# Up products of a ConvFFN: the convolution's accumulators in PSUM, another order at the entrance, and a product's low part moved from GpSimd to VectorE

## The reference

```
h2 = rmsnorm(x1) * (1 + sc2) + sh2              # 576 x 2048
u  = h2 @ w_up                                  # 576 x 11264
uc = depthwise_conv3(u_hist) + b_dw_f           # 3 taps, history in front of each sequence
y  = x1 + gt2 * ((silu(gate) * val) @ w_down)   # gate, val = the two halves of uc
```

## Time and profile before

| | us |
|---|---|
| median of 3 runs | 2999.72 |
| lowest and highest | 2998.53, 3000.04 |
| the profiled execution, its own time | 3009.53 |
| its span, first to last instruction | 3007.6 |

### The profile page before, as it was taken

The page is one execution under the profiler, slowest core; times in us unless marked ns, Lnnn a source line. Parts: engine busy times, 40 slices in busy tenths (PEclk is TensorE's granted clock), DMA queues, the critical chain, the costliest instruction groups (busy, mean ns, idle before and its releaser), DMA issues.

```text
span 3007.6 us, 52667 instructions
## 1 busy us (share of the span) xinstructions
PE 2814.1 (94%) x20368; PEld 2547.5 (85%) x20368; DVE 1940.0 (65%) x3011; ACT 1084.7 (36%) x2012; POOL 1708.9 (57%) x1894
## 2 busy tenths in 40 slices
PE   5798889999989879998899999999999989999999
PEld 2296478888964559997899999999999989999998
DVE  2225369999877543226888988998899843434342
ACT  2212323332214432125555555555555522121212
POOL 0134354444330064457799999999999954544453
PEclk8999999999989889998999999999999999999999
DMA  8832156552258683441333333333333453233323
GB/s 284 279 85 81 39 172 186 180 165 64 73 176 291 194 256 106 128 128 42 96 111 109 98 104 112 108 98 105 113 106 98 123 185 112 98 116 101 114 80 99
DMA packets 473921, 391.94 MB, mean 130 GB/s; under 512 B 29416, under 2 KB 402820, under 8 KB 473092
## 3 DMA queue, kind: packets, MB, share of 16 engines
q1 hardware_dynamic: 462914, 363.24, 39.4%
q0 software_dynamic: 8704, 19.27, 2.1%
q10 hardware_dynamic: 2075, 6.34, 0.7%
HBM read 363.85 MB, written 25.66 MB: 130 GB/s over the span
## 4 chain that ended last, share of the span: by engine, by line
PE 58%; POOL 19%; DVE 12%; DMA 4%; issue 3%; ACT 3%; ACTq 0%; SPq 0%; DVEq 0%; POOLq 0%
PE ps L1976 17%; POOL wlo L926 16%; PE ps L1428 15%; PE ps L2008 14%; DMA raw<-in_w_ada 3%; PE ps L1462 3%; DVE yb L2274 2%; DVE ye L2277 2%; POOL wlo L931 2%; POOL wlo L877 1%; ACT whi L1294 1%; DVE prod L2258 1%; DVE scP L2185 1%; PE ps L1887 1%; PE ps L1840 1%
## 5 line engine op out<-in xcount | busy, mean ns | idle before, releaser
L926 POOL TENSOR_TENSOR wlo<-raw,whi 128x256 fp32r<-128x256 f32 x672 | 764.0, 1169 | 82.6 <-ACT whi L1294 82.5
L877 POOL TENSOR_TENSOR wlo<-raw,whi 128x256 fp32r<-128x256 f32 (+1 forms) x424 | 370.3, 904 | 482.8 <-ACT whi L976 482.8
L931 POOL TENSOR_TENSOR wlo<-raw,whi 128x256 fp32r<-128x256 f32 x352 | 277.0, 819 | 296.3 <-ACT whi L1318 296.3
L2008 PE MATMUL ps<-XH,whi 128*128 128x288 f32 x1344 | 409.6, 305 | 15.2 <-POOL wlo L926 10.0
L1428 PE MATMUL ps<-XH,whi 128*128 128x288 f32 (+1 forms) x1760 | 390.7, 303 | 18.2 <-POOL wlo L877 16.8
L2008 PE MATMUL ps<-XH,wlo 128*128 128x288 f32 x1344 | 398.1, 296 | 0.0
L2008 PE MATMUL ps<-XL,whi 128*128 128x288 f32 x1344 | 398.0, 296 | 0.0
L2008 PE MATMUL ps<-x1R,whi 128*128 128x288 f32 x1344 | 396.5, 295 | 0.0
L1428 PE MATMUL ps<-XL,whi 128*128 128x288 f32 (+1 forms) x1760 | 378.6, 296 | 0.0
L1428 PE MATMUL ps<-XH,wlo 128*128 128x288 f32 (+1 forms) x1760 | 378.2, 296 | 0.0
L1294 ACT ACTIVATE whi<-raw 128x512 fp32r<-128x512 f32 x420 | 263.9, 629 | 269.3 <-PE ps L2008 178.9
(11 more groups left out here) (379 smaller groups left out, 6348.2 us busy)
## 6 DMA issues: line engine op xcount, KB each, us to landing
raw<-in_w_ada SPq DMA_DIRECT2D x192, 512.0 KB, 4.8
raw<-in_w_up SPq DMA_DIRECT2D x176, 512.0 KB, 4.0
raw<-in_w_down SPq DMA_DIRECT2D x88, 512.0 KB, 3.4
raw<-in_w_in SPq DMA_DIRECT2D x68, 512.0 KB, 5.4
Vp<-in_cache_v POOLq DMA_DIRECT2D x128, 128.0 KB, 4.0
raw<-in_w_out SPq DMA_DIRECT2D x32, 512.0 KB, 3.9
raw<-in_cache_k SPq DMA_DIRECT2D x64, 128.0 KB, 2.3
g32a<-g_far SPq DMA_DIRECT2D x6, 1152.0 KB
```

The costliest lines, as they stand in the source:

```text
L877: last = G.tensor_tensor(l[:, a:a + width // 4], raw_of(u, m)[:, a:a + width // 4], h[:, a:a + width // 4].bitcast(F32), ALU.subtract)
L926: last = G.tensor_tensor(lp[:, a:a + 256], src[:, a:a + 256], hp[:, a:a + 256].bitcast(F32), ALU.subtract)
L931: last = G.tensor_tensor(wlo[:, d % 2, a:a + 256], raw[:, d % 4, a:a + 256], whi[:, d % 2, a:a + 256].bitcast(F32), ALU.subtract)
L2008: ins = mm(dst, wt, x(4 * h + k), start=h + k == 0 and wt is a and x is xh, stop=h == 1 and k == 3 and wt is b)
```

## The change

- The accumulators of the convolution move from SBUF (`four`) to PSUM: two banks for v = 0 (4 and 5), two for v = 1 (6 and 7). The last tap of the gate row goes from PSUM to SBUF (`vals`), where Silu and the gate read it; the value row is read by the gate from PSUM.
- The seven products now share banks 0 to 3, so `product` waits for other readers. The copy p5 of product 1 is gone: VectorE reads bank 1.
- The low part of product 6 moves from GpSimd to VectorE, between `gate_rows` and `gate`. The count of GpSimd's low parts per pair goes from 10 to 8 halves wherever it is waited for.
- At the entrance ScalarE makes the high parts 6 and 7 of the plain products ahead of the evacuations, VectorE's `operand_forms` wait until GpSimd has made the low part 7, the first high half of product 0 goes ahead of the copies of the forms, and SyncE loads slots 0, 1, 2, 3 in this order.
- Left out below: the same change of counts in two waits of SyncE and one of TensorE, and other bank numbers in the state rows, the down stage and the output's transposes (the down stage's first tile now uses banks 0 and 1, with a wait for the last value rows).

```diff
-        p5 = at(o_c + 8 * TB + TB // 2, "p5", [128, TH])
...
-        gout = [four[:, 2 * CV:2 * CV + T], rstd[:, :]]
+        gout = [four[:, CV:CV + T], four[:, CV + T:CV + 2 * T]]
...
-        conv = [four[:, v * CV:v * CV + CV - 2] for v in range(2)]
+        vals = four[:, 0:CV - 2]
...
+        def conv(v):
+
+            return ps_all[:, 4 + 2 * v:6 + 2 * v, :].rearrange("p a c -> p (a c)")[:, 0:CV - 2]
...
-        POOL_LO, DVE_LO = (0, 2, 3, 5, 6), (1, 4)
+        POOL_LO, DVE_LO = (0, 2, 3, 5), (1, 4, 6)
...
             if p in DVE_LO:
-                return s_lod.at(4 * i + 2 * DVE_LO.index(p) + h + 1)
-            return s_lo, W0 + 10 * i + 2 * POOL_LO.index(p) + h + 1
+                return s_lod.at(6 * i + 2 * DVE_LO.index(p) + h + 1)
+            return s_lo, W0 + 8 * i + 2 * POOL_LO.index(p) + h + 1
...
-            for s in (3, 2, 0, 1):
+            for s in range(4):
                 block(0, s)
...
             def taps(f, v):
                 ch = f + v * FT
-                w(act, s_gt, f)
+                if v:
+                    w(act, s_gt, f)
+                elif f:
+                    act.wait_ge(s_c3, conv_count(f - 1, 0))
                 bias, tap = vT[:, 2, ch:ch + 1], vT[:, 5, ch:ch + 1]
-                A.activation(conv[v], cin[:, v, 0:CV - 2], ACT.Identity, bias=bias, scale=tap).then_inc(s_t0, 1)
+                A.activation(conv(v), cin[:, v, 0:CV - 2], ACT.Identity, bias=bias, scale=tap).then_inc(s_t0, 1)
                 last_rows_of(f, v)
...
-            def snap(i, which):
-
-                act.wait_ge(*product_done(i, which))
+            def snap(i):
+
+                act.wait_ge(*product_done(i, 0))
                 if i:
-                    act.wait_ge(*(s_u4 if which else s_c11).at(i))
-                    if which:
-                        act.wait_ge(*s_cv[1].at(i))
-                A.activation((p1, p5)[which][:, :], bank(which, 128, 0, TH), ACT.Copy).then_inc(s_snap.sem, 1)
+                    act.wait_ge(*s_c11.at(i))
+                A.activation(p1[:, :], bank(0, 128, 0, TH), ACT.Copy).then_inc(s_snap.sem, 1)
...
-                A.activation(conv[0], conv[0], ACT.Silu).then_inc(s_gl, 1)
+                A.activation(vals, vals, ACT.Silu).then_inc(s_gl, 1)
...
             hi(u, 4, 2)
+            hi(u, 6)
             up_evac(u, 2, 0, 0, 0)
+            hi(u, 7)
+            up_evac(u, 3, 0, 0, 1)
             silu_gate(0)
-            up_evac(u, 3, 0, 0, 1)
-            hi(u, 6)
-            hi(u, 7)
             up_evac(u, 5, 0, 1, 0)
-            act.wait_ge(s_form.sem, s_form.done + 4)
+            form_hi(0, 0, 0)
+            act.wait_ge(*s_form.at(3))
             form_rows(0, x1T[:, 0:8, 0:TH], T1h[:, :, :])
-            form_hi(0, 0, 0)
+            act.wait_ge(*s_form.at(4))
             form_rows(1, x1T[:, 8:16, 0:TH], T4h[:, :, :])
             silu_gate(1)
...
-                snap(i, 0)
+                snap(i)
...
-                snap(i, 1)
...
-                dst = bank((0, 1, 2, 3, 6, 7, 4)[p], 128, 0, TH)
-                if p < 2:
-                    pe.wait_ge(*(s_snap.at(2 * i - 1 + p) if i else (s_uv, 3)))
+                dst = bank((0, 1, 2, 3, 0, 3, 2)[p], 128, 0, TH)
+                if p == 0:
+                    pe.wait_ge(*(s_q.at(2 * i) if i else (s_uv, 3)))
+                elif p == 1:
+                    pe.wait_ge(*(s_u4.at(i) if i else (s_uv, 3)))
                 elif p == 2:
-                    pe.wait_ge(*(s_cv[1].at(i) if i else (s_uv, 4)))
+                    pe.wait_ge(*(s_cv[0].at(i) if i else (s_uv, 4)))
+                elif p == 3:
+                    w(pe, *s_c11.at(i))
+                elif p == 4:
+                    pe.wait_ge(*s_snap.at(i + 1))
                 elif p == 5:
-                    w(pe, *s_c11.at(i))
-                elif p == 6:
-                    w(pe, *s_cv[0].at(i))
+                    pe.wait_ge(*s_q.at(2 * i + 1))
+                else:
+                    pe.wait_ge(*s_cv[1].at(i + 1))
                 if i == 0 and 1 <= p <= 4:
...
             def operand_forms():
 
+                dve.wait_ge(s_lo, Tally(U_FFN).index(7) + 1)
                 TT(b11, b12, b11, ALU.subtract).then_inc(s_form.sem, 1)
...
-                link(STT(conv[v], cin[:, v, 1:CV - 1], tap(1), conv[v], ALU.mult, ALU.add))
-                STT(conv[v], cin[:, v, 2:CV], tap(2), conv[v], ALU.mult, ALU.add).then_inc(s_c3, 1)
+                link(STT(conv(v), cin[:, v, 1:CV - 1], tap(1), conv(v), ALU.mult, ALU.add))
+                if v == 0:
+                    w(dve, s_gt, f)
+                STT(conv(1) if v else vals, cin[:, v, 2:CV], tap(2), conv(v), ALU.mult, ALU.add).then_inc(s_c3, 1)
...
-                sample = [four[:, v * CV + 2 + SEQ:v * CV + CV].rearrange("p (b t) -> p b t", b=DB)[:, :, 0:DS] for v in range(2)]
-                TT(gout[f % 2][:, 0:SEQ], conv[0][:, 0:SEQ], conv[1][:, 0:SEQ], ALU.mult)
+                sample = [ap.rearrange("p (b t) -> p b t", b=DB)[:, :, 0:DS]
+                          for ap in (four[:, 2 + SEQ:CV], bank(7, 128, 2, 2 + DB * (2 + DS)))]
+                TT(gout[f % 2][:, 0:SEQ], vals[:, 0:SEQ], bank(6), ALU.mult)
                 TT(by8(gout[f % 2][:, SEQ:T]), sample[0], sample[1], ALU.mult).then_inc(s_gt, 1)
...
             def late_sum(i):
 
                 dve.wait_ge(*product_done(i, 3))
-                dve.wait_ge(*s_snap.at(2 * i + 1))
-                link(TT(u2[:, :], p1[:, :], bank(3, 128, 0, TH), ALU.add))
+                dve.wait_ge(*s_snap.at(i + 1))
+                TT(u2[:, :], p1[:, :], bank(3, 128, 0, TH), ALU.add).then_inc(s_q.sem, 1)
+                dve.wait_ge(*s_q.at(2 * i + 1))
 
             def gate_rows(i):
 
                 dve.wait_ge(*product_done(i, 4))
-                TT(up[:, 1, 2:2 + TH], u2[:, :], bank(6, 128, 0, TH), ALU.add).then_inc(s_q.sem, 1)
-                dve.wait_ge(*s_q.at(i + 1))
-                dve.wait_ge(*s_snap.at(2 * i + 2))
-                TT(up[:, 1, 2 + TH:], up[:, 1, 2:2 + SEQ - TH], p5[:, 0:SEQ - TH], ALU.add)
-                link(TT(us[:, 1, :, 2:], by8(up[:, 1, 2 + SEQ - TH:2 + TH]), by8(p5[:, SEQ - TH:TH]), ALU.add))
+                TT(up[:, 1, 2:2 + TH], u2[:, :], bank(0, 128, 0, TH), ALU.add).then_inc(s_q.sem, 1)
+                dve.wait_ge(*s_q.at(2 * i + 2))
+                TT(up[:, 1, 2 + TH:], up[:, 1, 2:2 + SEQ - TH], bank(1, 128, 0, SEQ - TH), ALU.add)
+                link(TT(us[:, 1, :, 2:], by8(up[:, 1, 2 + SEQ - TH:2 + TH]), by8(bank(1, 128, SEQ - TH, TH)), ALU.add))
                 TT(up[:, 1, 2:2 + TH], up[:, 1, 2:2 + TH], bank(2, 128, 0, TH), ALU.add).then_inc(s_cv[1].sem, 1)
 
             def value_rows(i, second):
 
                 if not second:
+                    TT(u2[:, :], u2[:, :], bank(1, 128, 0, TH), ALU.add).then_inc(s_u4.sem, 1)
                     dve.wait_ge(*product_done(i, 5))
-                    TT(up[:, 0, 2:2 + TH], p1[:, :], bank(7, 128, 0, TH), ALU.add).then_inc(s_c11.sem, 1)
-                    TT(u2[:, :], u2[:, :], p5[:, :], ALU.add).then_inc(s_u4.sem, 1)
+                    TT(up[:, 0, 2:2 + TH], p1[:, :], bank(3, 128, 0, TH), ALU.add).then_inc(s_c11.sem, 1)
                 else:
                     dve.wait_ge(*product_done(i, 6))
                     dve.wait_ge(*s_u4.at(i + 1))
-                    TT(up[:, 0, 2 + TH:], u2[:, 0:SEQ - TH], bank(4, 128, 0, SEQ - TH), ALU.add)
-                    TT(us[:, 0, :, 2:], by8(u2[:, SEQ - TH:TH]), by8(bank(4, 128, SEQ - TH, TH)), ALU.add).then_inc(s_cv[0].sem, 1)
+                    TT(up[:, 0, 2 + TH:], u2[:, 0:SEQ - TH], bank(2, 128, 0, SEQ - TH), ALU.add)
+                    TT(us[:, 0, :, 2:], by8(u2[:, SEQ - TH:TH]), by8(bank(2, 128, SEQ - TH, TH)), ALU.add).then_inc(s_cv[0].sem, 1)
...
                 gate_rows(i)
+                lo(i, 6)
                 gate(f - 1)
```

More of the change, by code:

```diff
@@ L838, in _ @@
                     if d >= 4:
-                        sp.wait_ge(s_lo, W0 + 10 * NU + d - 3)
+                        sp.wait_ge(s_lo, W0 + 8 * NU + d - 3)
                         sp.dma_start(raw[:, d % 4, :].rearrange("p (k n) -> p k n", n=256),
@@ L1311, in y_rows @@
                 w(act, s_yo[n % 4], 32 * (n // 4))
-                A.activation(yst[n % 4], bank(n % 2), ACT.Copy)
+                A.activation(yst[n % 4], bank(6 + n % 2), ACT.Copy)
                 A.activation(yss[:, n % 4, :], bank(4 + n % 2, NS, 0, 128), ACT.Copy).then_inc(s_ye, 1)
@@ L1333, in fo_rows @@
                 act.wait_ge(s_foo[par], (g - par) * 32 + 16)
-                A.activation(foS[:, par, :], bank(5, 128, 0, 128), ACT.Copy)
-                A.activation(foP[:, par, :], bank(5, 16, 128, 256), ACT.Copy).then_inc(s_foe, 3)
+                A.activation(foS[:, par, :], bank(5, 128, 128, 256), ACT.Copy)
+                A.activation(foP[:, par, :], bank(5, 16, 256, 384), ACT.Copy).then_inc(s_foe, 3)
             act.wait_ge(s_up0, 1)
@@ L1955, in state_rows @@
                 pe.wait_ge(s_foe, 3 * g + 1)
```

(16 more changed lines are left out.)

## The result

The changed kernel takes 2960.79 us (median of 4 runs, 2960.34 to 2967.38), the kernel before 2999.12 (4 runs); the ratio is 0.9874, with a 95% interval of 0.9857 to 0.989. The forecast was 2972, its range 2963 to 2990: the direction and the place were right, the gain of 38.3 us is larger than forecast, and the time lies 2.2 us under the low end of the range, which is within what medians of a few runs scatter. The kernel before was measured again beside the experiments: 3001.50 us beside 1 to 4, 2999.08 beside 5 to 8, 2998.87 beside 9 to 12; the ratios refer to these. One run of experiment 6 took 3108.56 us at a granted clock of 0.83, against 0.97 in all others, and is left out of its median.

A forecast was written before the change was run, and what follows sets the result against it. TensorE was taken as the floor, with the ring through ScalarE and GpSimd lengthening each pair to 23.08 us. Savings of 21.5 (steady part) and 6 (entrance), 27.5 us off the median 2999.72, gave 2972 us, range 2963 to 2990.

The forecast's parts named there:

- the entrance's dear end of 9: Entrance before the up products: upper bound of its net saving, 9 us, where 6 was forecast.
- step 1 of the steady part: Up products: GpSimd loses product 6, twelve instructions become eight at 1.167 us; the ring falls to 19.9 us, under 22.4.
- the ring: Cycle in each pair: ScalarE high half 0.64, GpSimd's twelve instructions 12.45, TensorE's six halves 9.86; with 0.13 between, 23.08 us.
- The steady part: Up-product pairs: 25.6 us that TensorE leaves, less 41 pairs x 0.1 = 4, giving 21.5 us saved.
- Step 6: Product 0's raw block may land late, leaving 0.1 us a pair, bounds 0 and 0.4.
- The entrance: Stage before the up products: waits of 3.27 and 5.16 us go, some waits are added; net 6 us saved, bounds 2 and 9.
- Step 2: VectorE in each pair: two low parts add 2.45 us, operands in PSUM save 3.2; 20.8 falls to 20.0 us.
- The rival of dear PSUM: VectorE's taps and additions get no cheaper in PSUM: 24.0 us a pair, 3032 us; 8% for slower, 5% for the same.
- VectorE at 20.0 us and GpSimd at 18: Expected work a pair in the changed profile: VectorE some 20 us, GpSimd 16 instructions in 18 us or less.
- Disturbed prices: Costs of VectorE operations beside busy GpSimd; gate rows to first addition takes 5.0 us, against 3.8 undisturbed.
- steps 4 and 5: TensorE's waits for reused banks are met; VectorE's delayed additions leave product 3 0.8 us in hand or 0.5 late, taken as 0.
- the additions' chain: Rival: VectorE's order from gate rows to product 3, or the landing, bounds pairs at 22.8 to 22.9 us: 2985 us, 25%.

The follow-up runs named there:

- experiment 6: Changed kernel with ScalarE making product 0's second high half ahead of form T4h's copy and the Silu at the entrance: 2963.17 us (three runs), ratio 0.9869.
- experiment 5: Changed kernel with SyncE sending the state rows of every fourth pair after issuing slot 0's block instead of ahead of it: 2960.31 us.
- experiment 7: Changed kernel with product 6's low part on GpSimd, state rows after slot 0, and product 0's second high half first: 2956.9 us, ratio 0.986.
- experiment 9: Changed kernel with product 6's low part on GpSimd and the SBUF copy p5 of product 1 back, taps staying in PSUM: 2963.85 us, ratio 0.9886.
- experiment 11: Changed kernel with state rows after slot 0 and product 0's second high half first, product 6's low part staying on VectorE: 2958.82 us.
- experiment 12: Same kernel as experiment 7 (product 6's low part on GpSimd), measured on the same chip as the changed kernel: 2960.92 us.
- experiment 4: Changed kernel with the old order at the entrance: 2968.27 us, ratio 0.9881.
- experiment 10: Changed kernel run and profiled again, with no edit: 2962.83 us.
- experiment 1: Changed kernel with only product 6's low part given back to GpSimd: 2962.22 us, ratio to before 0.9865.
- experiment 2: Kernel before with only product 6's low part moved to VectorE; accumulators and p5 in SBUF, old entrance: 3008.58 us, ratio 1.003.

## Why the prediction was wrong

**In size, the step that failed is the first: "TensorE's weight loads fill 927.37 of 953 us, and so 25.6 us are all that TensorE leaves", and "weight loads 22.43 of it (168 loads of 0.1335 us each, the pace)".** The floor is 22.31 us a pair. A load lasts 0.19 us and the next starts 0.133 later, so busy time counts a tail of nearly 0.06 behind the last load ahead of each gap, and a gap of 0.38 in the earlier trace rows costs 0.44. At 0.1328 us a load the 6955 loads of the earlier trace rows need 923.6 us, and 29.4 were left. 25.6 and the entrance's dear end of 9 make 2965 us; the forecast had little room below that. **In mechanism, it is step 1 of the steady part**: it gave the gain to the ring's eight instructions instead of twelve, and the runs show that the move of the low part has no share in it (below).

- *The steady part*: 21.5 forecast, 26.4 measured between product 1 and the down stage (28.7 in the second profile of the changed kernel). The 40 pairs from the second to the last gave 26.6 in both. At the floor (894.6 us, experiments 5, 7, 9, 11 and 12) these 40 pairs had 28.7 to give, so the room was 3.1 us larger than the 25.6 (the window of the earlier trace rows holds a little more than these pairs). Step 6 left 0.1 us in every pair for a late landing, 4 us; 2.1 stayed, and not in every pair: they are the breaks in three of ten state-row pairs, whose block waited on SyncE's queue (experiment 5).
- *The entrance*: 6 forecast, 7.5 measured up to product 1; up to the second pair 5.8 in the first profile of the changed kernel and 8.2 in the second. The waits of 3.27 and 5.16 us went, the evacuation's wait grew (0.41 to 1.41 us), and the gap at product 0's second half grew from 1.85 to 3.43 where I had 2.8: behind the Silu, as experiment 6 confirms. The forecast had one thing hidden in a sum: with the old order PSUM alone gives 3.6 up to product 1 (experiment 4). It had no term for the clock: behind the 3.43 us TensorE runs at a granted clock of 0.50 for 3.3 us, and in one of the two profiles once more.
- *Behind the products* I put nothing; 1.5 us came (588.3 to 586.8). The other profiles have 585.0 to 588.5, whatever the kernel, so this is within their scatter.
- *The rest* of the 38.3 us is 2.9 against the first profile of the changed kernel, which ran 5.6 us at the lower clock, and 0.2 against the second, which did not. How much of it is the clock and how much the scatter of medians is not shown; ahead of the mark the same program took up to 14 us more (experiment 10), so whether the median falls just under the range or just inside it is luck.
- *Step 2, the prices in PSUM*: right to 0.02 us for the tap and the additions. The rival of dear PSUM fell: 0.44 us with PSUM against 0.63 with SBUF, beside GpSimd. The Trainium skill ("VectorE: DVE Perf Modes", section on the TRN2 errata) charges PSUM 120 cycles against 58 and would have made these operations dearer; beside GpSimd this trace has them cheaper.
- *Step 1, the cause*: wrong. I let the ring go from twelve to eight instructions at the old price of 1.167 and gave the move the gain. Experiment 1 has twelve instructions and no loss, experiment 2 has eight and a loss. The gain is the price's: with VectorE's accumulators in PSUM GpSimd's 1.167 became 0.92 and VectorE's low half of product 1 0.92 instead of 1.225 (experiment 1). The ring of twelve at 0.89 is 12 x 0.89 + 10.63 = 21.3 us, under 22.31. The prediction names the ports that the two engines take from each other as a reason for a price, and does not carry it to the operations that stay; the runs show the prices, and the ports as their reason are argued.
- *VectorE at 20.0 us and GpSimd at 18*: measured 17.1 and 14.2, for the same reason. "Disturbed prices" were my doubt in steps 4 and 5; no wait of these steps stopped TensorE in the four pairs above.
- *The rivals*: the additions' chain is real and bounds the pair at 23.31 us where the accumulators stay in SBUF (experiment 2); in the changed kernel it does not appear.

## What to carry to other kernels

A floor is not read from busy time in a stretch that has gaps: take it from the pitch, start to start, in a run without one. Where VectorE and GpSimd work side by side, the price of each is partly the other's work; an edit that moves a VectorE operand to PSUM is to be costed for both engines, and may be worth more than moving instructions from one to the other. And try such an edit in its parts: here the move of a low part, alone a loss, rode along in a change that did not need it.

## What the runs showed of the hardware

- Beside GpSimd, VectorE's operations with two SBUF inputs are dear, also short ones: 64 columns take 0.749 us and 0.214 with one operand in PSUM; GpSimd's own 256 columns range from 0.739 us on the mean (experiment 1, on `sums`) to 1.167. The Trainium skill ("SBUF — State Buffer", two separate sides) has the two engines share a port pair under an exclusive lock for the whole instruction; these rows agree with it, though none shows the lock itself.
- A scalar-tensor-tensor of VectorE that reads and writes PSUM with a second tensor in SBUF runs at 0.83 us for 592 columns beside a working GpSimd, as the SBUF form does only alone.
- TensorE keeps 0.1328 us a matmul of 288 columns with its weight load (89.24 us for 672) through runs of four pairs at a granted clock of 1.00, the 2.4 GHz level.
- After a wait of 3.43 us at the entrance TensorE ran at a granted clock of 0.50, the 1.2 GHz level, for 3.3 us. After waits of 2.6 and 1.1 us it did so for 5.6 us in one execution of the changed kernel (24 weight loads where there were 43) and not in another.
